# Low parts of four output-projection weight tiles made by DVE behind each feature tile's input parts, instead of by POOL

## Chip, cores and metric

One Trainium2 chip, one core. The metric is the device time of the kernel in microseconds (us), one launch.

## What is computed

One step of an encoder layer on 544 tokens (512 of new streams, 32 of running ones), D = 1024, all in float32: an input projection, sliding-window attention and gated linear attention, a merge, an output projection with a residual, then a SwiGLU feed-forward with a second residual. Cut to what matters here:

```python
def _merge(x, oa, ob, rb, ga, gb, g_ob, w_out):
    ob = _rmsnorm(ob, g_ob).reshape(B, T, D_MODEL) * jax.nn.silu(rb)
    m = jax.nn.sigmoid(ga) * oa + jax.nn.sigmoid(gb) * ob
    return x + m @ w_out                      # the output projection: the stage of the change

def _ffn(x, g, w_gate, w_up, w_down):
    h = _rmsnorm(x, g)
    return x + (jax.nn.silu(h @ w_gate) * (h @ w_up)) @ w_down
```

## The kernel before

Activations are kept transposed (features on the 128 partitions, 544 tokens along the free dimension). Every float32 product is made of three fast ones: each operand is split into a high part (fp32r) and a low part (what the rounding left), and TensorE adds high x high, high x low and low x high (function `chunk`, lines 654 to 656). A weight tile is 1024 x 128, stored as 128 x 1024. Tiles are numbered in the order of use: 0 to 52 are the input projection, 53 to 60 (`OUT0` = 53) the output projection, and from 61 (`GU0[0]`) come gate and up tiles in pairs for the feed-forward, whose products go by a scheme of sums of halves (`gate_up`, `first_gate_up`), and then down tiles.

A weight tile goes through a ring of 4 slots (`RING`): SyncE loads it into `wraw` (512 KB), ACT makes the high part `w_hi` (`high_part`, line 1066), and POOL or DVE makes the low part `w_lo` = `wraw` - `w_hi` (POOL in `lows`, line 594; DVE in `weight_low_part`, line 1786). Each low part adds 1 to the semaphore `w_split`. TensorE starts tile n when `w_split` is at least n + 1, and SyncE loads tile n only when the low part of tile n - 4 is counted (`raw_free`, line 445). So the load of tile 62, the first up tile, waits for the low part of tile 58. SyncE issues its loads in program order: 59, the residual rows of step 4, 60, residual 5, 61 (gate), residual 6, 62 (up), 63 (gate), residual 7, 64 (up).

DVE makes the low parts of tiles 4 to 33, POOL those of 1 to 3 and of 34 to 60 (and later of the down tiles).

The order of DVE's and ACT's work is written out by hand. In the output projection, step t (0 to 7) takes weight tile 53 + t and gives feature tile i = 0, 4, 1, 5, 2, 6, 3, 7 of the new residual x2T. On DVE a step is: add the residual to the PSUM result (line 1974), which also frees the PSUM bank; make the combinations for the feed-forward (`ffn_input`); and subtract ACT's high part (`f_low_part`, which waits for ACT twice in odd steps and once in even ones, and then counts `f_ok`). Even steps (i < 4) also add squares into `rv` (`add_squares`, line 1851). Step 4 begins, behind its residual add, with `first_sum(0)` (line 1892): it adds the two halves of up tile 62, so it waits for that load. From its result a chain runs over POOL's queue: an accumulating DMA (line 608), a second one (line 613), then ACT's high part of the sums (line 1097, in ACT's order behind step 5), then DVE's low part of them in step 6 (line 1903). Step 5 ends with a low part of tile 61, step 6 with `first_sum(1)`, step 7 holds the low part of tile 62.

TensorE goes through the eight tiles and then through `first_gate_up`: it starts when `f_ok` is 7, runs what needs the first seven feature tiles, and waits for `f_ok` = 8 before the rest.

Of the kernel before, what the change touches and what calls it, by code (L numbers as in the profile page):

```python
# [58 lines left out]
RING = 4  # L59
# [34 lines left out]
OUT0 = N_IN  # L94
OUT_ORDER = [0, 4, 1, 5, 2, 6, 3, 7]
FF_GROUPS = [8, 7, 7]
GU0, DN0 = [], []
# [30 lines left out]
def gemms(n):  # L128

    return sum(m not in PAIR_OF for m in range(n))  # L130


def uses_before(n):

    return sum(USES[m] for m in range(n % 2, n, 2))
# [12 lines left out]
HANDOVER = UNIT0 + 4  # L148
# [39 lines left out]
def mixer_program(nc, x_prompt, x_sample, cache_k, cache_v, state, w_in, w_a2, b_a, g_q, g_k, sinks,  # L188
                  g_ob, w_out, g_mix, g_ffn, w_gate, w_up, w_down,
                  y_prompt, y_sample, nk_p, nv_p, ns_p, nk_s, nv_s, ns_s):  # L190
    with ExitStack() as ctx:
        def sem(name):
            return ctx.enter_context(nc.semaphore(name))
# [141 lines left out]
        def halves(ps):  # L335

            return ps[:, :].rearrange("p (b n) -> p b n", b=2)[:, :, 0:TH]

        def h2(ap):

            return ap.rearrange("p (b n) -> p b n", b=2)
# [3 lines left out]
        w_split = sem("w_split")  # L345
# [228 lines left out]
        @block.gpsimd  # L574
        def _(pool):
            pool.memset(ident[:, :], 0.0).then_inc(pool_step, 1)
            pool.memset(cmask[:, :], 1.0).then_inc(pool_step, 1)
            pool.wait_ge(pool_step, 2)
            pool.affine_select(out=ident[:, :], in_=ident[:, :], compare_op=ALU.not_equal, fill=1.0,
                               base=0, pattern=[[-1, P]], channel_multiplier=1).then_inc(const_pool, 1)  # L580

            pool.iota(dist[:, :], pattern=[[-1, 2 * P]], base=P, channel_multiplier=1,
                      allow_small_or_imprecise_dtypes=True).then_inc(const_pool, 1)

            pool.affine_select(out=cmask[:, :], in_=cmask[:, :], compare_op=ALU.is_ge, fill=0.0,
                               base=0, pattern=[[1, P]], channel_multiplier=-1).then_inc(pool_step, 1)
            pool.wait_ge(pool_step, 3)
            cm = cmask[:, :].rearrange("p (b n) -> p b n", b=4)
            pool.affine_select(out=cm, in_=cm, compare_op=ALU.is_ge, fill=0.0, base=0,
                               pattern=[[-32, 4], [0, 32]], channel_multiplier=1).then_inc(const_pool, 1)  # L590

            def low_part(slot):

                pool.tensor_tensor(w_lo[:, slot, :, :], wraw[:, slot, :, :],  # L594
                                   w_hi[:, slot, :, :].bitcast(F32), ALU.subtract).then_inc(w_split, 1)

            def low_rank_low_part():

                pool.wait_ge(hi_done, 1)
                pool.tensor_tensor(w_hi[:, 0, :, RANK:2 * RANK], wraw[:, 0, :, 0:RANK],  # L600
                                   w_hi[:, 0, :, 0:RANK].bitcast(F32), ALU.subtract).then_inc(w_split, 1)

            def first_sums(q):

                r1 = (PAIRS[q][1] + 1) % RING
                pool.wait_ge(neg_ok, q + 1)
                pool.wait_ge(s1_ok, q + 1)
                pool.dma_start(wraw[:, r1, 0:HK, :], csum[q % 2][:, 1], accum_op=ALU.add).then_inc(s3_ok[q % 2], 16)  # L608

            def second_sum(q):  # L610

                pool.wait_ge(s3_ok[q % 2], 16 * (q // 2 + 1))
                pool.dma_start(csum[q % 2][:, 1], csum[q % 2][:, 0], accum_op=ALU.add).then_inc(s2_ok[q % 2], 16)

            def last_sum(q):

                pool.wait_ge(neg4_ok, q + 1)
                pool.wait_ge(s2_ok[q % 2], 16 * (q // 2 + 1))
                pool.dma_start(csum4[q % 2][:, :, :], csum[q % 2][:, 1], accum_op=ALU.add).then_inc(s4_ok, 16)

            def lows(ns):
                for n in ns:
                    pool.wait_ge(hi_done, gemms(n + 1))
                    low_part(n % RING)

            low_rank_low_part()
            lows(range(1, RING))
            pool.wait_ge(w_split, HANDOVER)
            lows(range(HANDOVER, GU0[0]))
            for g, m in enumerate(FF_GROUPS):  # L630
                q0 = FIRST[g]
                first_sums(q0)
                second_sum(q0)
                last_sum(q0)
                first_sums(q0 + 1)
                second_sum(q0 + 1)
                for q in range(q0, q0 + m):
                    if q + 2 < q0 + m:
                        first_sums(q + 2)
                    if q + 1 < q0 + m:  # L640
                        last_sum(q + 1)
                    if q + 2 < q0 + m:
                        second_sum(q + 2)
                lows(range(DN0[g], DN0[g] + KC))
# [824 lines left out]
        def _(dve):  # L1469
            steps = [0]  # L1470

            def link(ins):

                steps[0] += 1
                ins.then_inc(dve_step, 1)
                dve.wait_ge(dve_step, steps[0])
# [304 lines left out]
            def weight_low_part(m):  # L1781
                s = m % RING
                dve.wait_ge(hi_done, m + 1)
                if m == RING:
                    dve.wait_ge(w_split, RING)
                dve.tensor_tensor(w_lo[:, s, :, :], wraw[:, s, :, :], w_hi[:, s, :, :].bitcast(F32),  # L1786
                                  ALU.subtract).then_inc(w_split, 1)

# [8 lines left out]
            for n in range(N_IN):  # L1797
                if n == gate_tile(HEADS_B - 1) + 1:
                    empty_rows()
                if RING <= n + 2 < HANDOVER:  # L1800
                    weight_low_part(n + 2)
# [69 lines left out]
            def f_low_part(t, c):  # L1871
                dve.wait_ge(fin_ok, t + 1)
                if c < HK:
                    dve.wait_ge(f_hi_ok, t + 1)
                    dve.tensor_tensor(fa_lo[:, c], fin[:, 0:2], fa_hi[:, c].bitcast(F32), ALU.subtract)\
                        .then_inc(f_ok, 1)
                    return
                dve.wait_ge(f01_hi_ok, c - HK + 1)
                link(dve.tensor_tensor(fb_lo[:, c - HK, 0:2], fin[:, 0:2], fb_hi[:, c - HK, 0:2].bitcast(F32),
                                       ALU.subtract))  # L1880
                dve.wait_ge(f_hi_ok, t + 1)
                dve.tensor_tensor(fb_lo[:, c - HK, 2:5], fin[:, 2:5], fb_hi[:, c - HK, 2:5].bitcast(F32),
                                  ALU.subtract).then_inc(f_ok, 1)

            def first_sum(q):

                r1 = (PAIRS[q][1] + 1) % RING
                dve.wait_ge(wload[r1], 32 * ((PAIRS[q][1] + 1) // RING + 1))
                if q >= 2:
                    dve.wait_ge(pair_lo, 3 * (q - 1))  # L1890
                    dve.wait_ge(s2_ok[q % 2], 16 * (q // 2))
                dve.tensor_tensor(csum[q % 2][:, 0], wraw[:, r1, 0:HK, :], wraw[:, r1, HK:KC, :], ALU.add)                    .then_inc(s1_ok, 1)  # L1892

            def low_parts(q, k, at=None):

                _, n = PAIRS[q]
                dve.wait_ge(pair_hi, 3 * q + (k if at is None else at) + 1)
                if k < 2:
                    r = (n + k) % RING
                    lo, raw_w, hi = w_lo[:, r], wraw[:, r], w_hi[:, r]  # L1900
                else:
                    lo, raw_w, hi = c_lo[q % 2][:, :], csum[q % 2][:, :], c_hi[q % 2][:, :]
                dve.tensor_tensor(lo, raw_w, hi.bitcast(F32), ALU.subtract).then_inc(pair_lo, 1)  # L1903
# [66 lines left out]
            for t, i in enumerate(OUT_ORDER):  # L1970
                n = OUT0 + t
                dve.wait_ge(gemm_done, n + 1)
                dve.wait_ge(in_xres[t % XTS], 16 * (t // XTS + 1))
                dve.tensor_tensor(h2(x2T[:, i, :]), halves(G[n % 2]), h2(xTi[:, t % XTS, :]), ALU.add)\
                    .then_inc(set_free[n % 2], 1)
                dve.wait_ge(set_free[n % 2], uses_before(n) + 1)
                if t == HK:
                    first_sum(0)
                if t == 6:
                    low_parts(0, 2, 1)  # L1980
                if t == KC - 1:
                    low_parts(0, 1, 2)
                if i < HK and t:
                    add_squares(t - 1)
                ffn_input(i)
                f_low_part(t, i)
                if i < HK:
                    add_squares(t)
                if t == 5:
                    low_parts(0, 0)  # L1990
                if t == 6:
                    first_sum(1)
# [96 lines left out]
```

## Time and profile before

| | |
|---|---|
| median of 3 runs | 895.72 us (894.04 to 898.93) |
| the profiled execution, its own time | 896.06 us |
| span in the profile | 894.0 us |
| TensorE clock granted, mean | 0.998 |
| busy, share of span | PE 98%, weight load 95%, DVE 65%, ACT 46%, POOL 22% |

A timeline row has the start in us from the span's start, the duration, engine, line, operation, output and input, and in brackets how long the engine had been idle before and who released it. TensorE's matmuls are pipelined: one starts each 0.126 us though each is shown at 0.29 us. Two DVE instructions that don't depend on each other overlap by some 0.08 us, so the next one can start before the row's end. "busy (x)" in a table of windows is busy time and number of instructions.

### The profile page before, as it was taken

To read this page: it belongs to the slowest core of one execution; us is meant where nothing else is said; L and a number is where in the kernel's file an instruction comes from. 1 tells how busy PE (TensorE), PEld (TensorE's weight loads), DVE (VectorE), ACT (ScalarE), POOL (GpSimd) and SP (SyncE) were. 2 spreads that over 40 slices of the span, in tenths; PEclk is the share of its full clock that TensorE was granted. 3 is DMA by queue.
4 is the path that set the end of the run, shared out by engine and by line. 5 is a ranking of instruction groups with operands and counts; after the bars stand their busy time and mean duration, and the time that the engine had idled before them with its cause. 6 is when DMAs were issued, how large, how long until landed. Compare 5 with 4: busy or idle time off the path is not lost.

```text
span 894.0 us, 17248 instructions
## 1 busy us (share of the span) xinstructions
PE 875.1 (98%) x7061; PEld 848.2 (95%) x7061; DVE 579.7 (65%) x1156; ACT 414.0 (46%) x757; POOL 197.3 (22%) x131
## 2 busy tenths in 40 slices
PE   8989999999999999999999989999999999999998
PEld 7989999989998999999999989999999999999997
DVE  6773666676885436565556899973379853699722
ACT  6732443534554454545444575542155541366421
POOL 2200000000002323232324213235122153222350
PEclk9999999999999999999999999999999999999999
DMA  8531222121523121212107469853288723888322
GB/s 277 154 90 53 67 76 71 48 83 40 138 71 95 49 71 49 73 48 72 48 25 207 118 131 194 177 147 97 69 191 180 168 85 100 173 177 164 94 80 63
DMA packets 151028, 96.38 MB, mean 108 GB/s; under 512 B 5008, under 2 KB 140646, under 8 KB 150822
## 3 DMA queue, kind: packets, MB, share of 16 engines
q1 hardware_dynamic: 136326, 74.96, 29.3%
q0 software_dynamic: 9504, 17.31, 12.5%
q10 hardware_dynamic: 5120, 3.02, 1.2%
q8 instruction: 56, 0.92, 0.4%
q14 instruction: 22, 0.18, 0.1%
HBM read 71.45 MB, written 5.83 MB: 86 GB/s over the span
## 4 chain that ended last, share of the span: by engine, by line
PE 85%; DVE 9%; ACT 3%; issue 2%; DMA 2%; POOL 0%; DVEq 0%; SPq 0%; POOLq 0%
PE G L654 17%; PE G L656 16%; PE G L655 16%; PE X L933 4%; PE X L935 4%; PE X L936 4%; PE G L933 4%; PE G L935 4%; PE G L936 4%; PE X L864 2%; PE X L848 2%; PE X L833 2%; PE X L786 1%; PE X L774 1%; DVE w_lo L1786 1%
## 5 line engine op out<-in xcount | busy, mean ns | idle before, releaser
L654 PE MATMUL G<-h_hi,w_hi 128*128 128x272 f32 x1280 | 381.4, 298 | 3.4 <-DVE vB L1678 1.9
L656 PE MATMUL G<-h_hi,w_lo 128*128 128x272 f32 x1280 | 370.8, 290 | 0.0
L655 PE MATMUL G<-h_lo,w_hi 128*128 128x272 f32 x1280 | 369.2, 288 | 0.0
L654 PEld LDWEIGHTS G<-h_hi,w_hi 128*128 128x128 f32 x1280 | 241.6, 189 | 11.0 <-issue 7.0
L655 PEld LDWEIGHTS G<-h_lo,w_hi 128*128 128x128 f32 x1280 | 241.8, 189 | 0.8
L594 POOL TENSOR_TENSOR w_lo<-wraw,w_hi 128x1024 fp32r<-128x1024 f32 x54 | 138.4, 2570 | 470.7 <-DVE w_lo L1786 247.2
L656 PEld LDWEIGHTS G<-h_hi,w_lo 128*128 128x128 f32 x1280 | 241.3, 189 | 0.0
L1066 ACT ACTIVATE w_hi<-wraw 128x1024 fp32r<-128x1024 f32 (+1 forms) x129 | 134.5, 1045 | 60.6 <-PE G L656 35.2
L1266 ACT ACTIVATE prob<-prob,nm 128x256 f32<-128x256 f32 (+2 forms) x80 | 36.7, 460 | 64.4 <-DVE sd L1719 64.4
L2054 DVE TENSOR_TENSOR rs<-G,rv 128x544 f32<-128x544 f32 x23 | 16.7, 725 | 75.6 <-PE G L656 75.6
L1393 ACT ACTIVATE sq<-sq 128x544 f32<-128x544 f32 x22 | 14.5, 658 | 98.9 <-DVE sq L1941 98.9
L1903 DVE TENSOR_TENSOR w_lo<-wraw,w_hi 128x1024 fp32r<-128x1024 f32 x44 | 53.4, 1217 | 0.5 <-ACT w_hi L1066 0.5
L608 POOL DMA_DIRECT2D wraw<-csum x22 | 19.6, 889 | 111.5 <-DVE csum L1892 105.7
L933 PE MATMUL X<-fb,w_hi 128*128 128x272 f32 x144 | 41.5, 288 | 1.3 <-DVE up L1922 1.3
L935 PE MATMUL X<-fb,w_hi 128*128 128x272 f32 x144 | 41.5, 288 | 0.0
L936 PE MATMUL X<-fb,w_lo 128*128 128x272 f32 x144 | 41.5, 288 | 0.0
L1786 DVE TENSOR_TENSOR w_lo<-wraw,w_hi 128x1024 fp32r<-128x1024 f32 x30 | 36.3, 1216 | 2.7 <-ACT w_hi L1066 2.5
L933 PE MATMUL G<-fb,w_hi 128*128 128x272 f32 x120 | 34.8, 290 | 0.3 <-DVE up L1922 0.3
L935 PE MATMUL G<-fb,w_hi 128*128 128x272 f32 x120 | 34.7, 289 | 0.0
L936 PE MATMUL G<-fb,w_lo 128*128 128x272 f32 x120 | 34.6, 288 | 0.0
L1903 DVE TENSOR_TENSOR c_lo<-csum,c_hi 128x1024 fp32r<-128x1024 f32 x22 | 26.8, 1218 | 6.3 <-ACT c_hi L1097 6.2
L1726 DVE TENSOR_TENSOR den<-sm,es 128x4 f32<-128x4 f32 (+1 forms) x20 | 3.2, 160 | 41.8 <-ACT es L1268 41.8
(322 smaller groups left out, 1819.2 us busy)
## 6 DMA issues: line engine op xcount, KB each, us to landing
wraw<-in_w_in_dram SPq DMA_DIRECT2D x52, 512.0 KB
wraw<-in_w_gate_dram SPq DMA_DIRECT2D x22, 512.0 KB
wraw<-in_w_up_dram SPq DMA_DIRECT2D x22, 512.0 KB
csum<-csum POOLq DMA_DIRECT2D x44, 256.0 KB, 5.2
wraw<-in_w_down_dram SPq DMA_DIRECT2D x16, 448.0 KB
wraw<-csum POOLq DMA_DIRECT2D x22, 256.0 KB, 3.5
wraw<-in_w_out_dram SPq DMA_DIRECT2D x8, 512.0 KB
wraw<-in_w_down_dram SPq DMA_DIRECT2D x8, 512.0 KB
```

The costliest lines, as they stand in the source:

```text
L594: pool.tensor_tensor(w_lo[:, slot, :, :], wraw[:, slot, :, :], w_hi[:, slot, :, :].bitcast(F32), ALU.subtract).then_inc(w_split, 1)
L608: pool.dma_start(wraw[:, r1, 0:HK, :], csum[q % 2][:, 1], accum_op=ALU.add).then_inc(s3_ok[q % 2], 16)
L654: pe.matmul(o, w_hi[:, slot, kc, :], b_hi[:, kc, cols], start=(kc == 0), stop=False)
L655: pe.matmul(o, w_hi[:, slot, kc, :], b_lo[:, kc, cols], start=False, stop=False)
L656: mm = pe.matmul(o, w_lo[:, slot, kc, :], b_hi[:, kc, cols], start=False, stop=(kc == last))
L933: pe.matmul(bank, a_hi[:, kc, :], b_hi[:, kc, :], start=(kc == 0 and not adds), stop=False, skip_group_check=adds)
L935: pe.matmul(bank, a_hi[:, kc, :], b_lo[:, kc, :], start=False, stop=False, skip_group_check=adds)
L936: mm = pe.matmul(bank, a_lo[:, kc, :], b_hi[:, kc, :], start=False, stop=(kc == HK - 1), skip_group_check=adds)
L1066: act.activation(w_hi[:, n % RING, :, 0:m], wraw[:, n % RING, :, 0:m], ACT.Copy)\
L1266: act.activation(prob[0:nq, s, i, lo:hi], prob[0:nq, s, i, lo:hi], ACT.Exp, bias=nm[0:nq, s, i:i + 1], accum_out=sm[0:nq, s, i:i + 1])
L1786: dve.tensor_tensor(w_lo[:, s, :, :], wraw[:, s, :, :], w_hi[:, s, :, :].bitcast(F32), ALU.subtract).then_inc(w_split, 1)
L1903: dve.tensor_tensor(lo, raw_w, hi.bitcast(F32), ALU.subtract).then_inc(pair_lo, 1)
```

## The change

DVE makes the low parts of tiles 55 to 58 (steps 2 to 5), each two steps ahead of its use: behind `f_low_part` of step t it makes the one of tile 55 + t, for t = 0 to 3. POOL keeps 53 and 54, waits until `w_split` has counted 59, and then makes 59 and 60. DVE waits once, at tile 55, for POOL's count of 55, so that the counts keep their order.

```diff
@@ pool: order of the low parts
             pool.wait_ge(w_split, HANDOVER)
-            lows(range(HANDOVER, GU0[0]))
+            lows(range(HANDOVER, OUT0 + 2))
+            pool.wait_ge(w_split, OUT0 + 6)
+            lows(range(OUT0 + 6, GU0[0]))
@@ dve: weight_low_part
                 dve.wait_ge(hi_done, m + 1)
-                if m == RING:
-                    dve.wait_ge(w_split, RING)
+                if m in (RING, OUT0 + 2):
+                    dve.wait_ge(w_split, m)
@@ dve: for t, i in enumerate(OUT_ORDER)
                 ffn_input(i)
                 f_low_part(t, i)
+                if t < 4:
+                    weight_low_part(OUT0 + t + 2)
                 if i < HK:
                     add_squares(t)
```

## Rows read from the trace of the kernel before

**Rows 1.** The page: busy time of each engine
```profile
PE 875.1 (98%) x7061; PEld 848.2 (95%) x7061; DVE 579.7 (65%) x1156; ACT 414.0 (46%) x757; POOL 197.3 (22%) x131
```

**Rows 2.** Busy time by stretch (us; engine, busy, count; PEclk, DMA share, GB/s)
```profile
470.00:512.50 42.50, 42.50 (x340) 42.50 (x340) 30.92 (x45) 22.41 (x33) 14.03 (x8) 1.00 0.63 166
520.00:536.00 16.00, 14.00 (x103) 12.96 (x101) 15.29 (x25) 11.18 (x16) 2.58 (x3) 1.00 0.57 125
488.00:488.50 0.50, 0.50 (x6) 0.50 (x5) 0.00 (x0) 0.00 (x0) 0.50 (x1) 1.00 0.03 9
```

**Rows 3.** The chain that ended last, at the end of the first pair
```profile
520.86 0.71 DVE rv L1851
```

**Rows 4.** Timeline of TensorE: first matmul of steps 2, 3, first_gate_up, and the last part
```profile
476.37 0.29 PE L654 MATMUL G<-e_hi,w_hi 128*128 128x272 f32 x1
...
482.40 0.29 PE L654 MATMUL G<-e_hi,w_hi 128*128 128x272 f32 x1
...
512.57 0.29 PE L933 MATMUL G<-fa_hi,w_hi 128*128 128x272 f32 x1
...
518.98 0.28 PE L933 MATMUL G<-fb,c_hi 128*128 128x272 f32 x1
```

**Rows 5.** Timeline of POOL: low parts of tiles 56, 58, 59, 60, then a sum by DMA
```profile
468.98 2.44 POOL L594 TENSOR_TENSOR w_lo<-wraw,w_hi 128x1024 fp32r<-128x1024 f32 x1 [7.53 <-ACT w_hi L1066]
...
481.85 2.40 POOL L594 TENSOR_TENSOR w_lo<-wraw,w_hi 128x1024 fp32r<-128x1024 f32 x1 [3.67 <-ACT w_hi L1066]
487.44 2.70 POOL L594 TENSOR_TENSOR w_lo<-wraw,w_hi 128x1024 fp32r<-128x1024 f32 x1 [3.20 <-ACT w_hi L1066]
493.90 2.40 POOL L594 TENSOR_TENSOR w_lo<-wraw,w_hi 128x1024 fp32r<-128x1024 f32 x1 [3.76 <-ACT w_hi L1066]
497.46 1.00 POOL L608 DMA_DIRECT2D wraw<-csum  x1 [1.15 <-DVE csum L1892]
```

**Rows 6.** Instructions of line 1786, DVE's weight low parts: min/median/max ns
```profile
L1786 DVE TENSOR_TENSOR w_lo<-wraw,w_hi x30: 1197/1218/1226, 37.7 to 273.7; 128x1024 fp32r<-128x1024 f32 x30
```

**Rows 7.** Timeline of DVE in the output projection: ahead of step 0, and steps 0 to 7
```profile
469.08 2.36 DVE L1969 TENSOR_SCALAR param<-param 128x8 f32<-128x8 f32 x1
471.48 0.72 DVE L1974 TENSOR_TENSOR x2T<-G,xTi 128x544 f32<-128x544 f32 x1
...
476.57 0.72 DVE L1974 TENSOR_TENSOR x2T<-G,xTi 128x544 f32<-128x544 f32 x1 [1.48 <-PE G L656]
...
480.92 1.01 DVE L1882 TENSOR_TENSOR fb<-fin,fb 128x816 fp32r<-128x816 f32 x1 [0.26 <-ACT fb L1371]
482.61 0.72 DVE L1974 TENSOR_TENSOR x2T<-G,xTi 128x544 f32<-128x544 f32 x1 [0.68 <-PE G L656]
483.36 1.47 DVE L1851 TENSOR_TENSOR rv<-rv,sq 128x544 f32<-128x544 f32 x1
...
487.16 0.72 DVE L1851 TENSOR_TENSOR rv<-rv,sq 128x544 f32<-128x544 f32 x1
...
495.43 1.42 DVE L1892 TENSOR_TENSOR csum<-wraw 128x512 f32<-128x512 f32 x1
...
500.70 0.72 DVE L1974 TENSOR_TENSOR x2T<-G,xTi 128x544 f32<-128x544 f32 x1 [0.17 <-PE G L656]
...
507.11 0.72 DVE L1974 TENSOR_TENSOR x2T<-G,xTi 128x544 f32<-128x544 f32 x1
...
517.71 1.01 DVE L1882 TENSOR_TENSOR fb<-fin,fb 128x816 fp32r<-128x816 f32 x1 [0.26 <-ACT fb L1371]
```

**Rows 8.** Timeline of SyncE's queue: loads of tiles 57 and 58, and of 62
```profile
468.33 1.37 SPq L527 DMA_DIRECT2D wraw<-in_w_out_dram  x2
...
484.27 0.39 SPq L527 DMA_DIRECT2D wraw<-in_w_up_dram  x1
```

**Rows 9.** ACT in steps 0 and 5: a high part that waited for its load, and of the sums
```profile
474.62 1.06 ACT L1066 ACTIVATE w_hi<-wraw 128x1024 fp32r<-128x1024 f32 x1 [0.71 <-DMA wraw<-in_w_out_dram]
...
505.80 1.04 ACT L1097 ACTIVATE c_hi<-csum 128x1024 fp32r<-128x1024 f32 x1
```

## The prediction, made before the changed kernel had run

> **What bounds the kernel.** I read the page first, then busy time by stretch, the chain, and the timelines of the five queues in the 60 us in which the change works. TensorE is busy 98% of the span [rows 1], and in the output projection, from step 1 on, it is busy all of 42.50 us [rows 2]: no low part is late there, whoever makes it. After it the state changes: between 520 and 536 TensorE is busy 14.00 of 16 us and DVE 15.29 [rows 2], and from 520.86 the chain runs over DVE [rows 3]. So this stage has two clocks. TensorE takes a step in 482.40 - 476.37 = 6.03 us [rows 4]; DVE, with its waits for ACT, needs a little less in the first steps (idle 0.68 us before step 2) and hardly less later (0.17 before step 5, nothing before step 6) [rows 7]. DVE hands over to TensorE at `f_ok` = 8: its last instruction of step 7 ends at 517.71 + 1.01 = 518.72, TensorE reaches that point at 518.98 [rows 4, 7]. Only 0.26 us in hand; what makes DVE later than that moves the end, and as the chain stays with DVE behind it, nothing there takes it back.
>
> **What POOL loses.** Four low parts of 2.4 to 2.75 us. Nobody waits for them, so by itself this gives nothing. One effect on DVE is visible: a DVE instruction with its inputs in SBUF that meets a POOL low part lasts until that ends. The squares' sum at 483.36 took 1.47 us where 487.16 took 0.72, and POOL's ended at 484.25; the tiny one at 469.08 took 2.36 until POOL's end at 471.42; `first_sum(0)` took 1.42 until 496.85, POOL's ended at 496.30, so 0.55 after it [rows 5, 7]. The first two stretches vanish. They were in front of waits, so nothing is gained at the end (costed below).
>
> **What DVE gains: four low parts of 1.22 us [rows 6], effectively 1.14 in a row of instructions.**
> - Tile 55, behind step 0. Step 0 starts at 471.48 or earlier, its last input part ends by 474.7, so the low part ends by 475.9; step 2 needs it at 476.37 [rows 4, 7]. Cost 0. DVE was idle 1.48 us before step 1, which pays for it.
> - Tile 56, behind step 1. The input parts are through at 480.92 + 0.92 = 481.84, the low part ends at 483.05. TensorE's step 3 should begin at 482.40: it waits, with 0.1 for the start, **0.75 us**. DVE begins step 2 at 482.95 instead of 482.61.
> - Tile 57, behind step 2. An even step took 487.16 - 482.61 = 4.55, with the 0.75 that POOL held it; without, 3.8. So 482.95 + 3.8 + 1.2 = 487.95; TensorE needs it at 482.40 + 6.03 + 0.75 = 489.2. Cost 0.
> - Tile 58, behind step 3. An odd step takes 481.84 - 476.57 = 5.27. It starts when TensorE ends step 3, now 489.4; so 494.65 + 1.2 = 495.85 against a need at 495.2: again **0.75 us**. TensorE is now 1.5 behind.
>
> The waits at `hi_done` and at `w_split` = 55 are met long before, and POOL's 59 (from 495.9) and 60 (from 498.3), 2.4 each, are done at 498.3 and 500.7, ahead of steps 6 and 7 (502.0 and 508.0). Cost 0.
>
> **What the counts move on SyncE's queue.** The load of tile 62 waits for the low part of tile 58, today issued at 484.27, right when POOL ends (484.25) [rows 5, 8]. Now that low part ends at 495.85: the load goes out **11.6 us later**. Today's had its bytes moved by 488.0 with residual rows beside it, at most 3.7 us [rows 2, 8]; alone I take 3.3, so it lands at 499.2. Loads 59, 60, 61 are later too, but each lands before its high part; 63 and 64 go out at 498.4 and 500.8, needed at 511 and 517. The one who waits for tile 62 is DVE, at `first_sum(0)`, with all of steps 4 to 7 queued behind it.
>
> **Step 4.** DVE's residual add starts at 495.75 and needs no wait. Then it stands until 499.2, when POOL is in the middle of the low part of tile 60 and keeps the port until 500.7. `first_sum(0)` ends 0.55 later at 501.25 instead of 496.85: **4.4 us late**. The price of the landing lies between 3.0 us (then POOL's hold decides anyway) and the 6.2 that tile 57's load took from 468.33 to its high part at 474.6 behind four residual loads [rows 8, 9]; any landing between 498.7 and 500.7 gives the same time, and I take it for that reason.
>
> By the Trainium skill (SBUF — State Buffer, Who interferes with whom) whichever of DVE and GpSimd starts first holds the shared ports for its whole instruction and the other fully blocks. The rows agree; without the hold the sum would be 1.4 less, one of the rivals.
>
> **Steps 5 to 7.** Before step 5 DVE was idle 0.17 us and before 6 and 7 not at all, so the 4.4 shrinks by 0.17 and by a little where ACT had been the later one: step 5 starts at 504.85 (500.70), step 6 at 511.2 (507.11), the last input part ends at 522.8 (518.72), **+4.1**. The DMA chain on POOL's queue moves as one: line 608 from 497.46 to 501.9 (+4.4), so the high part of the sums in ACT's order from 505.80 to about 510, and step 6 needs its result at 512: 1 us to spare, which also covers ACT's queue behind that wait. TensorE ends step 7 1.5 late, stands some 2.3 us for `f_ok` = 7, works, and meets `f_ok` = 8 at 522.8 + 0.2 = 523.0 instead of 518.98: **+4.0 us**. The 1.5 lies inside this, not on top. `first_sum(1)` moves by 4.1 as well, so the next pair starts its sums no earlier relative to the rest.
>
> **Sum.** 0 (POOL) + 4.0 = 4.0 us. The profiled execution took 896.06 (span 894.0, 2.06 around it), so it would be 900.1; against the median of 895.72, which is 0.34 lower, 899.7: +0.45%. What a measurement here can tell from no change is about 0.5%, or 4.5 us, so this is **within it, on the slow side**.
>
> **Rivals.**
> 1. *Slower beyond 0.5%: the load of tile 62 lands after POOL's hold ends.* Place: `first_sum(0)`. Below 500.7 it costs nothing more; from there each us is one us at the end, and past +0.5 it leaves the band. With the 6.2 us of tile 57's load it lands at 502.05, the sum ends at 502.7, 5.9 late: +5.5 at the end, 901.2. For it: the load of 63 and residual rows follow it from 498.4. Against it: at its issue nothing is ahead of it in the queue, and today's took at most 3.7.
> 2. *Not held.* POOL and DVE slip past each other at 499.2, so `first_sum(0)` ends at 499.85: +2.6, 898.3. If the load were no wait at all, DVE would catch up with TensorE and only the two waits for tiles 56 and 58 stay: +1.5, 897.2. For it: small shifts decide who has the port. Against it: all three meetings in the rows were holds, and the load can't leave before 495.85.
> 3. *Faster, because the port is no longer shared.* DVE gets back 2.3 + 0.75 us, and a DVE instruction is half of POOL's. Were that on the path, it would give 895.72 - 3.0 = 892.7, and even this needs TensorE waiting for DVE before 512.5, where it had no idle at all. On the gains of this kind the Trainium skill (GPSIMD Engine Reference, Elementwise) has elementwise work with two inputs about twice as fast on VectorE. The trace agrees, 1.22 against 2.40, but at a place where nobody waits.
>
> **How the numbers follow.** The forecast 0.60, rival 1 0.17, rival 2 0.20, rival 3 0.03. The forecast's own spread, some 0.5 us of working and as much of measurement about +4.0, lies over 4.5 in 4 cases of 10: 0.24 to slower, 0.36 to within. So slower 0.17 + 0.24 = 0.41, rounded 0.40; faster 0.03; within 0.57. The range goes from the low end of rival 2, less 0.2 (897.0), to rival 1 with 1 us over it (902.2).
>
> **What would show it.** Right: four instructions of line 1786 between 474 and 496; TensorE idle some 0.75 us before steps 3 and 5, released by DVE's low part; the up load issued near 496; DVE idle about 3 us before `first_sum(0)`, and that instruction long, until POOL's end plus 0.55; TensorE idle about 2.3 us before `first_gate_up`; from there everything 4.0 later, with equal gaps. Wrong: no DVE idle at `first_sum(0)`; a load that lands after POOL; a gap behind 536 that closes or grows, which would say that the delay is taken back or paid again.

## The result, and the profile after the change

The changed kernel took a median of 902.08 us (898.94 to 903.63, 8 runs) against 896.52 (894.04 to 898.93, 8 runs) for the kernel before: the ratio is 1.0058, with a 95% interval of 1.0046 to 1.0070. By the ratio that is 5.2 us, 4.1 to 6.3. The forecast was +4.0 us, within 0.5% and "on the slow side", with 899.7 us and a range of 897.0 to 902.2. The time lies inside the range, near its end. But the ratio is above the half per cent, where the forecast had put 0.40; its likelier outcome, within the half per cent (0.57), did not come.

The profiled execution of the changed kernel took 901.81 us with a span of 899.7, 5.7 more than the span before. The page gives the busy time of each engine:

```profile
PE 877.7 (98%) x7061; PEld 850.0 (94%) x7061; DVE 578.5 (64%) x1160; ACT 414.1 (46%) x757; POOL 186.8 (21%) x127
```

DVE has four instructions more, and yet 1.2 us less of busy time than in [rows 1]. The added ones take 4.9 us; against them stand four instructions that POOL's low parts had stretched by 5.8 us in all. Three of them are in [rows 7] (2.19, 0.75 and 0.73 us too long). The fourth lies earlier, beside the low part of tile 55, in DVE's timeline before:

```profile
459.22 2.81 DVE L1772 TENSOR_TENSOR obT<-obT,gaT 128x544 f32<-128x544 f32 x1
```

The same instruction takes 0.72 us elsewhere. Busy time alone would have called the change a gain.

Busy time by stretch (the columns are those of [rows 2]), first the second stretch before, then both after:

```profile
512.50:520.00 7.50, 7.50 (x62) 7.50 (x61) 6.26 (x10) 5.99 (x11) 1.70 (x2) 1.00 0.60 125
```
```profile
470.00:512.50 42.50, 41.40 (x327) 40.96 (x327) 28.83 (x43) 20.41 (x30) 7.44 (x5) 1.00 0.54 149
512.50:520.00 7.50, 5.37 (x43) 5.18 (x42) 6.61 (x11) 4.08 (x8) 0.85 (x1) 1.00 0.58 111
```

TensorE was never idle in these stretches before; now it is, 1.1 us in the first and 2.1 in the second. The timeline of TensorE shows the three places, steps 3 and 5 of the output projection and the start of `first_gate_up`:

```profile
483.12 0.39 PE L656 MATMUL G<-e_hi,w_hi 128*128 128x272 f32 x1 [0.56 <-DVE w_lo L1788]
...
495.99 0.39 PE L656 MATMUL G<-e_hi,w_hi 128*128 128x272 f32 x1 [0.55 <-DVE w_lo L1788]
...
516.48 0.36 PE L935 MATMUL G<-fa_hi,w_hi 128*128 128x272 f32 x1 [2.13 <-issue]
```

(The row's idle time is a little under the loss, since the first matmul of a restart is longer (0.39 us against 0.29): from the last matmul at 482.27 to 483.12 it lost 0.72 us beyond its pace of 0.126. Waits of TensorE that are given in the text without a row include this, some 0.16 us. The third row names no releaser; the count it waits for, `f_ok` = 7, comes from DVE's input part of step 6, which ended at 516.37.)

The timeline of DVE in steps 3 to 5:

```profile
494.71 1.22 DVE L1788 TENSOR_TENSOR w_lo<-wraw,w_hi 128x1024 fp32r<-128x1024 f32 x1
495.85 0.72 DVE L1976 TENSOR_TENSOR x2T<-G,xTi 128x544 f32<-128x544 f32 x1
500.68 0.69 DVE L1894 TENSOR_TENSOR csum<-wraw 128x512 f32<-128x512 f32 x1 [4.12 <-DMA wraw<-in_w_up_dram]
...
504.97 0.72 DVE L1976 TENSOR_TENSOR x2T<-G,xTi 128x544 f32<-128x544 f32 x1
```

Here is the turn of the case: DVE stands for 4.12 us, and `first_sum(0)` ends at 501.37 instead of 496.85, 4.5 us late; step 5 starts at 504.97 instead of 500.70 [rows 7]. SyncE's queue says why the load was not there. It was issued at 495.96 instead of 484.27 [rows 8], when the low part of tile 58 was counted:

```profile
495.96 0.39 SPq L527 DMA_DIRECT2D wraw<-in_w_up_dram  x1
498.44 0.39 SPq L527 DMA_DIRECT2D wraw<-in_w_gate_dram  x1
```

and POOL's two low parts, which met DVE's wait:

```profile
496.01 4.75 POOL L594 TENSOR_TENSOR w_lo<-wraw,w_hi 128x1024 fp32r<-128x1024 f32 x2 [42.09 <-DVE w_lo L1788]
```

To follow the delay across kernels whose start differs by up to 2 us, I use one **measure** from here on: from TensorE's restart at the end of its wait near 468 to its restart behind the last wait of the second pair, near 537. These are the restarts before, and then after:

```profile
467.95 0.39 PE L654 MATMUL G<-h_hi,w_hi 128*128 128x272 f32 x1 [0.78 <-DVE h_lo L1777]
...
537.39 0.36 PE L933 MATMUL X<-fb,c_hi 128*128 128x272 f32 x1 [1.77 <-DVE c_lo L1907]
```
```profile
467.97 0.39 PE L656 MATMUL G<-h_hi,w_hi 128*128 128x272 f32 x1 [0.76 <-DVE h_lo L1779]
...
541.55 0.36 PE L935 MATMUL X<-fb,c_hi 128*128 128x272 f32 x1 [1.77 <-DVE c_lo L1909]
```

In the kernel before it is 537.39 - 467.95 = 69.44 us, in the changed one 541.55 - 467.97 = 73.58: **+4.14**. The stretch behind the measure holds the rest of the 5.7. Windows of the changed kernel (PEclk is the third column from the right):

```profile
540.00:542.00 2.00, 0.45 (x3) 0.48 (x4) 2.00 (x5) 1.11 (x2) 0.66 (x2) 1.00 0.56 155
542.00:544.00 2.00, 2.00 (x14) 2.00 (x13) 2.00 (x3) 0.00 (x0) 1.07 (x2) 0.69 1.05 218
544.00:546.00 2.00, 2.00 (x11) 2.00 (x10) 1.24 (x4) 0.66 (x1) 0.84 (x1) 0.50 1.04 143
546.00:548.00 2.00, 2.00 (x17) 2.00 (x17) 1.63 (x3) 1.64 (x3) 0.00 (x0) 0.96 1.08 269
```

TensorE was granted half its clock, 1.2 instead of 2.4 GHz, from about 542.8 to 546.2, behind a stretch in which it had waited 1.44 and 1.93 us. In the profile before, after waits of the same size, it kept 1.00 at this place:

```profile
540.00:542.00 2.00, 2.00 (x19) 2.00 (x18) 1.24 (x4) 0.92 (x3) 0.84 (x1) 1.00 1.06 141
542.00:544.00 2.00, 2.00 (x19) 2.00 (x18) 1.97 (x3) 2.00 (x5) 0.00 (x0) 1.00 1.09 280
```

A later matmul, one near 600, moved from 600.63 to 606.31, by 5.68, against 4.16 at the measure's end: the stretch at half clock cost 1.5 us.

### The profile page after: what moved, and what is told of

It is laid out like the page before. It is cut to its first block, busy times and chain, and to the rows that moved or that the text cites. A ratio compares the mean times of both kernels' runs of the same rounds, so it can differ in the third digit from the quotient of the medians.

```text
span 899.7 us, 17250 instructions
## 1 busy us (share of the span) xinstructions
PE 877.7 (98%) x7061; PEld 850.0 (94%) x7061; DVE 578.5 (64%) x1160; ACT 414.1 (46%) x757; POOL 186.8 (21%) x127
## 4 chain that ended last, share of the span: by engine, by line
PE 77%; DVE 11%; DMA 4%; issue 3%; ACT 3%; SPq 1%; POOL 0%; DVEq 0%; POOLq 0%
PE G L656 15%; PE G L658 14%; PE G L657 14%; PE G L935 4%; PE G L937 4%; PE G L938 4%; PE X L935 4%; PE X L937 4%; PE X L938 4%; PE X L866 2%; PE X L850 2%; PE X L835 2%; DMA csum<-csum 1%; DMA wraw<-in_w_in_dram 1%; DVE w_lo L1788 1%
## 5 line engine op out<-in xcount | busy, mean ns | idle before, releaser
L594 POOL TENSOR_TENSOR w_lo<-wraw,w_hi 128x1024 fp32r<-128x1024 f32 x50 | 128.0, 2568 | 486.3 <-DVE w_lo L1788 289.3
L1905 DVE TENSOR_TENSOR w_lo<-wraw,w_hi 128x1024 fp32r<-128x1024 f32 x44 | 53.4, 1217 | 0.8 <-ACT w_hi L1068 0.8
L1788 DVE TENSOR_TENSOR w_lo<-wraw,w_hi 128x1024 fp32r<-128x1024 f32 x34 | 41.2, 1217 | 2.7 <-ACT w_hi L1068 2.5
```

## The experiments

The theory, from the prediction: the delay comes over the **late load** of tile 62, for which DVE waits with four steps behind it. Rivals: DVE has too much work; TensorE's own waits for low parts; POOL's hold; and, new after the result, the granted clock.

### One low part alone

Only tile 58 goes to DVE, all others stay with POOL:

```diff
-            lows(range(HANDOVER, OUT0 + 2))
+            lows(range(HANDOVER, OUT0 + 5))
             pool.wait_ge(w_split, OUT0 + 6)
@@ dve: weight_low_part
-                if m in (RING, OUT0 + 2):
+                if m in (RING, OUT0 + 5):
                     dve.wait_ge(w_split, m)
@@ dve, behind f_low_part
-                if t < 4:
+                if t == 3:
                     weight_low_part(OUT0 + t + 2)
```

> DVE makes only the low part of tile 58 (behind step 3); POOL makes all others. The mark is the first matmul behind TensorE's last wait in the first pairs, 537.39 us in the kernel before and 541.55 after the change. Theory 'late load' (the load of tile 62 waits for the low part of 58, DVE waits for that load): one low part is enough for nearly all of the delay. Load issued near 495.1, first_sum(0) ends near 500.4, mark at 540.5 (+3.2). Rival 'DVE is overloaded' (four times 1.14 us of work): a quarter of the delay, mark near 538.4 (+1.0). Rival 'TensorE's waits for low parts': one wait of 0.75, mark at 538.1.

Measured: 901.11 us (4 runs), ratio 1.0048 (1.0034 to 1.0062). The measure is 541.02 - 467.60 = 73.42, +3.98. A quarter of the work makes nearly all of the delay, which leaves no room for a price by the amount of work, and TensorE has only one of its two waits. The size was higher than I expected (3.2), as SyncE's and DVE's timelines show:

```profile
494.78 0.39 SPq L527 DMA_DIRECT2D wraw<-in_w_up_dram  x1
```
```profile
500.14 0.69 DVE L1894 TENSOR_TENSOR csum<-wraw 128x512 f32<-128x512 f32 x1 [4.75 <-DMA wraw<-in_w_up_dram]
```

The load went out at 494.78 and DVE went on at 500.14, 5.4 us later, and half a microsecond after POOL's last low part had ended (494.83 + 4.76 = 499.59). So here the landing, not POOL, ended the wait.

### The other three

DVE makes 55, 56 and 57, POOL 58 as soon as 57 is counted:

```diff
-            pool.wait_ge(w_split, OUT0 + 6)
-            lows(range(OUT0 + 6, GU0[0]))
+            pool.wait_ge(w_split, OUT0 + 5)
+            lows(range(OUT0 + 5, GU0[0]))
@@ dve, behind f_low_part
-                if t < 4:
+                if t < 3:
                     weight_low_part(OUT0 + t + 2)
```

> DVE makes the low parts of 55, 56 and 57, POOL that of 58 at once when 57 is counted. Late load: the load of 62 goes out near 490.5 and is there before DVE wants it; only the wait for tile 56 (0.75 us) and POOL's hold for tile 60 are left, mark between +0.5 and +0.8. DVE overloaded: three quarters of the delay, +3.1.

Measured: 898.88 us (9 runs), ratio 1.0024 (1.0013 to 1.0036); the measure is 539.96 - 468.26 = 71.70, +2.26. Neither theory had the number. The load was no longer the cause (issued at 491.22, DVE's `first_sum(0)` at 497.55 did not wait for it). The timeline of DVE shows what took its place:

```profile
491.56 2.28 DVE L1867 SCALAR_TENSOR_TENSOR fin<-x2T,param,fin 128x272 f32<-128x272 f32 x1 [1.07 <-ACT fin L1362]
...
497.55 2.21 DVE L1894 TENSOR_TENSOR csum<-wraw 128x512 f32<-128x512 f32 x1
```

The first of them takes 0.50 us elsewhere, the second 0.69. POOL, let go once the low part of 57 was counted, ran two low parts in a row (488.38, 5.17 us for both) into the middle of step 3, and the third met `first_sum(0)`. The first hold is 1.8 us and new, the second 1.5 where it was 0.7 before [rows 7]. They are not the whole of it. Counted from each kernel's restart near 468 (468.26 here, 467.95 before), DVE was already 0.8 us late when it began step 3 (489.76 against 488.64), because TensorE had waited 0.7 us for tile 56, and `first_sum(0)` ended 2.6 us late. So the holds added 1.8 of the 2.6 there (the rest of what they took went into idle time), and 2.26 reached the measure's end. Where POOL's instruction falls matters as much as how long it is.

### The same four, one step earlier

```diff
-                if t < 4:
-                    weight_low_part(OUT0 + t + 2)
+                for m in ((2, 3), (4,), (5,))[t] if t < 3 else ():
+                    weight_low_part(OUT0 + m)
```

> The same four low parts on DVE, 55 and 56 behind step 0, 57 behind step 1, 58 behind step 2. Late load: the load of 62 goes out near 488, no low part is late for TensorE, mark at 537.4 (0.0, within 0.3). DVE overloaded: the work is the same, so the delay stays at 3 to 4 us. If the granted clock's drop comes with chance from one execution to the next, the time equals that of the kernel before within 1.5 us.

Measured: 896.44 us (12 runs), ratio 0.9995 (0.9984 to 1.0006). The measure is 535.62 - 466.17 = 69.45, +0.01. SyncE's and DVE's timelines:

```profile
486.27 0.39 SPq L527 DMA_DIRECT2D wraw<-in_w_up_dram  x1
```
```profile
493.65 1.70 DVE L1894 TENSOR_TENSOR csum<-wraw 128x512 f32<-128x512 f32 x1
```

DVE makes the same four low parts and nothing is lost: the load of 62 goes out at 486.27 (488 as expected, since this execution is 1.8 us ahead of the kernel before at its restart near 468), no low part is late for TensorE, and POOL's last one meets `first_sum(0)` as it did before (1.70 us for it). So neither DVE's 4.9 us of work nor the exchange of engines costs anything by itself; together with tile 58 alone, this puts the cost on the moment at which the low part of tile 58 ends. Nor does the change gain anything where it is well placed.

### DVE's wait without POOL

The change, with tiles 59 and 60 made by DVE too, inside its own wait:

```diff
             lows(range(HANDOVER, OUT0 + 2))
-            pool.wait_ge(w_split, OUT0 + 6)
-            lows(range(OUT0 + 6, GU0[0]))
@@ dve
                 if t == HK:
+                    weight_low_part(OUT0 + 6)
+                    weight_low_part(OUT0 + 7)
                     first_sum(0)
```

> The change, and tiles 59 and 60 also made by DVE, in the 4 us in which it stands before first_sum(0); POOL makes none of 55 to 60, so it holds no port there. If POOL's hold set the end of the wait: first_sum(0) starts where the load lands, 499.4 to 499.6, mark 1.2 earlier than after the change, 540.3. If the load's landing set it (it lands at 500.6, 4.7 us after its issue): first_sum(0) starts at 500.6 as before, mark at 541.5.

Measured: 901.25 us (6 runs), ratio 1.0046 (1.0030 to 1.0063); measure 541.33 - 467.88 = 73.45, +4.01. DVE's timeline:

```profile
495.78 0.72 DVE L1974 TENSOR_TENSOR x2T<-G,xTi 128x544 f32<-128x544 f32 x1
496.53 2.36 DVE L1786 TENSOR_TENSOR w_lo<-wraw,w_hi 128x1024 fp32r<-128x1024 f32 x2
500.40 0.69 DVE L1892 TENSOR_TENSOR csum<-wraw 128x512 f32<-128x512 f32 x1 [1.51 <-DMA wraw<-in_w_up_dram]
```

With no POOL instruction anywhere near, `first_sum(0)` still starts at 500.40, 4.5 us after the issue at 495.89. The landing ends the wait. In the changed kernel POOL's last low part ended at 500.76 and `first_sum(0)`, started at 500.68, took its plain 0.69 us: it was not held, and POOL's end only happened to fall on the same moment. Two instructions of 1.2 us in that wait cost nothing, a second sign that DVE has time there.

### Four idle subtractions on top of the kernel before

```diff
                 f_low_part(t, i)
+                if t < 4:
+                    dve.tensor_tensor(csum[1][:, :].rearrange("p a k n -> p (a k n)"),
+                        e_hi[:, :, :].rearrange("p a n -> p (a n)")[:, 0:2 * TH + 480].bitcast(F32),
+                        e_lo[:, :, :].rearrange("p a n -> p (a n)")[:, 0:2 * TH + 480].bitcast(F32),
+                        ALU.subtract)
```

> The kernel before, POOL making all its low parts, and four extra subtractions of 128x1024 on DVE behind the input parts of steps 0 to 3, of the size of a low part, whose results nobody reads. Measure: from TensorE's restart at the end of its one wait near 468 to its restart behind the last wait near 537 (before 69.44 us; after the change 73.58). Late load: nothing waits for these four, the load of 62 goes out by 485.5; POOL's holds meet DVE more often, so +0.5 to +2.0. DVE overloaded: the same work as in the change, so +4.

The four results are read by nobody. Measured: 902.75 us (4 runs), ratio 1.0077 (1.0057 to 1.0097); the measure is 544.06 - 467.97 = 76.09, +6.65. I expected 0.5 to 2. DVE's timeline:

```profile
483.74 2.18 DVE L1851 TENSOR_TENSOR rv<-rv,sq 128x544 f32<-128x544 f32 x1
...
489.39 2.92 DVE L1851 TENSOR_TENSOR rv<-rv,sq 128x544 f32<-128x544 f32 x1
...
499.36 2.15 DVE L1892 TENSOR_TENSOR csum<-wraw 128x512 f32<-128x512 f32 x1
```

The extra work itself is small, but it makes DVE and POOL meet in every step: three instructions of about 0.7 us took 2.2, 2.9 and 2.15, together 5.1 us too long (two of them were held before, for 0.75 and 0.73, so 3.6 is new). The holding went both ways: POOL's low parts of tiles 58, 59 and 60 took 3.49, 3.19 and 3.48 us, where they took 2.40, 2.70 and 2.40 before [rows 5]. Step 5 began at 505.10, as late as in the changed kernel, though load 62 had gone out at 485.37. The granted clock was at half from about 515.4 to 522.2, in and behind a wait of TensorE of 4.0 us, and that is in the measure too. So this run doesn't show that DVE's work is harmless; it shows that extra work beside POOL's low parts costs as much as the late load. That four instructions of this size are harmless where they replace POOL's is what the earlier placement shows.

### The late load alone

The kernel before, one wait added on SyncE's queue:

```diff
                 gate_weights(0, i)
                 residual(XTS + 2 + i)
+                if i == 0:
+                    sp.wait_ge(f_ok, 4)
                 up_weights(0, i)
```

> The kernel before, POOL making all its low parts, with one wait more: SyncE issues the load of tile 62 only behind the input parts of step 3 (near 494). No work is added to DVE, no low part is late. Late load: this alone makes most of the delay; the load lands 4.4 to 5.8 us after its issue as in the changed kernels, first_sum(0) ends near 499.5 instead of 496.85, and TensorE's restart behind the last wait near 537 moves by 2.3 to 3.8 us against its restart near 468 (69.44 before, so 71.7 to 73.2). Rival (DVE's four instructions and TensorE's two waits are needed for it): no move beyond 0.5.

The wait holds back what SyncE issues behind it too: the load of 63 went out at 494.60 (490.17 before), followed by residual rows. Measured: 899.46 us (7 runs), ratio 1.0039 (1.0023 to 1.0055). No instruction moved between engines, no low part was late, and DVE stands as in the changed kernel. SyncE's and DVE's timelines:

```profile
494.16 0.39 SPq L527 DMA_DIRECT2D wraw<-in_w_up_dram  x1
```
```profile
499.81 0.69 DVE L1894 TENSOR_TENSOR csum<-wraw 128x512 f32<-128x512 f32 x1 [4.27 <-DMA wraw<-in_w_up_dram]
```

`first_sum(0)` ends at 500.50 instead of 496.85, 3.65 later. The measure is 542.01 - 468.10 = 73.91, +4.47, more than that, as the clock was at half behind the 2.9 us wait before `first_gate_up`:

```profile
514.00:516.00 2.00, 0.39 (x2) 0.42 (x3) 1.21 (x2) 1.97 (x3) 0.00 (x0) 0.92 0.00 0
516.00:518.00 2.00, 2.00 (x11) 2.00 (x11) 1.97 (x4) 0.73 (x3) 0.71 (x1) 0.50 0.03 8
518.00:520.00 2.00, 2.00 (x14) 2.00 (x14) 1.93 (x4) 1.84 (x4) 0.15 (x1) 0.73 0.75 112
```

What this costs can be read off. From the restart before `first_gate_up` to the measure's end, the changed kernel, the runs with tile 58 alone, with the other three and without POOL take 25.07 to 25.10 us; this run takes 542.01 - 515.61 = 26.40. So 1.3 us of the +4.47 are the clock and 3.2 the late load. That is 1.0 less than the +4.14 of the changed kernel, because the load went out 1.8 us earlier and took 0.9 longer. (With the idle subtractions the same stretch took 27.45: 2.4 of its +6.65 are the clock.) The late load is enough for the delay; the wait it makes is then a candidate for a slow clock.

### The clock: waits filled with idle matmuls

Each execution comes with its mean granted clock, and the times lie in steps with it. Of the kernel before, the comparisons with the experiments hold 61 executions: nine at 1.000 (median 894.67 us), 38 at 0.998 (896.52), ten at 0.996 (898.09), four others. The step from 1.000 to 0.998 is a stretch at half clock behind a 2 us wait near 55, which the profiles of both kernels have. These are the windows before:

```profile
58.00:60.00 2.00, 2.00 (x11) 2.00 (x11) 1.85 (x3) 1.99 (x4) 0.00 (x0) 0.54 0.44 134
60.00:62.00 2.00, 2.00 (x13) 1.99 (x12) 0.73 (x1) 0.22 (x1) 0.00 (x0) 0.61 0.04 10
```

The profiled execution of the earlier low parts, at a mean of 1.000, had the same wait and kept its clock:

```profile
58.00:60.00 2.00, 2.00 (x19) 1.99 (x18) 1.97 (x3) 1.93 (x3) 0.00 (x0) 1.00 0.26 78
```

The pair of waits at the end of the measure, 1.3 and 1.8 us in the rows, is the same in eight profiles in which nothing fills it. Behind it the clock fell in three (the changed kernel, tile 58 alone, the late load) and stayed up in five.

In 13 of 61 the clock of the kernel before was 0.996 or 0.995; in the changed one in six of eight. First the two waits of the second pair were filled in the changed kernel (`keep_busy` runs products of ones into columns that nobody reads):

```diff
+                if q == 1:
+                    keep_busy(G[0][:, 288:288 + P], 4)
                 pe.wait_ge(evicted, 6 * q + 2)
                 product(b7, w_hi[:, r1, k2], w_lo[:, r1, k2], fb_hi[:, :, 4], fb_lo[:, :, 4], adds=True)
+                if q == 1:
+                    keep_busy(G[0][:, 288:288 + P], 6)
                 pe.wait_ge(evicted, 6 * q + 3)
```

> The change, and 4 and 6 idle matmuls on TensorE into an unused part of a PSUM bank in its two waits of the second pair (near 536 and 540), shorter than the waits. Clock theory: part of the 5.2 us is no wait but the granted clock at half behind these waits, in most executions of the change and in a quarter of those of before; with the waits filled it does not fall there, the measure stays at +4.1, the mean granted clock rises from 0.996 to 0.998 or more, and the time falls by 1 to 1.6 us. Rival (the clock has nothing to do with it): time as after the change, 902.

Measured: 901.35 us (6 runs), ratio 1.0054 (1.0038 to 1.0070): inconclusive on the time. The measure was 544.27 - 468.23 = 76.04, +6.60 and not +4.1 as expected. The clock stayed at 1.00 from 536 to 548, but in this profile it was at half from about 519.2 to 522.7, behind the wait before `first_gate_up`, which was 3.4 us long here, since `first_sum(0)` started only at 502.04, 5.8 us after the load's issue. (The stretch from the restart at 517.84 to the measure's end took 26.43, so 1.3 us of it are the clock; the rest of what it has over the changed kernel is the longer landing.) Two executions at 0.999 took 899.31 (median), three at 0.997 901.76. So one stretch was avoided and another came in its place.

Then all waits filled, in three kernels. The fills of the second pair, and

```diff
+                if n == 5:
+                    pe.wait_ge(z_free, HEADS_B)
+                    keep_busy(X[1][:, 832:832 + P], 6)
                 if n >= 2:
                     pe.wait_ge(set_free[n % 2], uses_before(n))
```

on top of the early low parts and on top of the kernel before; and in the changed kernel also, ahead of `first_gate_up`,

```diff
+                keep_busy(X[0][:, 288:288 + P], 8)
                 pe.wait_ge(set_free[1], uses_before(n))
                 pe.wait_ge(f_ok, KC - 1)
```

> Low parts one step earlier (as in e3), the two waits of the second pair filled as in e7, and 6 idle matmuls in TensorE's 2 us wait near 55, behind which the granted clock is at half at 58 to 62 in most executions. Clock theory: mean granted clock 1.000, 894.4, which is what the undisturbed executions of e3 took; 2.4 less than the kernel before. Rival: the idle matmuls change nothing or delay what waits behind them, 896.4 or more.

> The kernel before with the same three fills. Clock theory: 894.4, as the executions of before at a mean clock of 1.000 (894.2). If the early low parts are worth nothing, e8 and e9 are equal within 0.3 us.

> The change with the fills of e8 and 8 idle matmuls more in the wait before first_gate_up (2.3 us). Clock theory: mean granted clock 0.999 or more, and against the filled kernel before (894.4) only the waits are left, 4.2 to 5: 898.5 to 899.4; so the clock had 2.5 to 3.5 us of the 902.1. Rival (no part of the clock): 900 to 901.5.

| kernel | median us (runs) | ratio to before, 95% | measure |
|---|---|---|---|
| early low parts, filled | 894.65 (11) | 0.9980 (0.9970 to 0.9989) | 69.44 |
| before, filled | 894.36 (11) | 0.9977 (0.9969 to 0.9986) | 69.45 |
| changed, filled | 898.96 (9) | 1.0031 (1.0019 to 1.0043) | 73.58 |

All executions of the three had a mean clock of 0.999 or 1.000. One execution of the first took 4823.73 us at a mean clock of 1.000, and nothing on record explains it; its ten others lie between 893.42 and 895.78, and the ratio is theirs. The wait near 55, filled in the kernel before:

```profile
54.68 1.50 PE L673 MATMUL X<-ones 128*128 128x128 f32 x12
56.61 0.40 PE L654 MATMUL G<-h_hi,w_hi 128*128 128x272 f32 x1 [0.43 <-DVE vB L1685]
```

(the row counts each of the six idle products twice), and its windows:

```profile
56.00:60.00 4.00, 3.57 (x29) 3.39 (x28) 3.81 (x8) 2.67 (x4) 0.00 (x0) 1.00 0.48 131
60.00:64.00 4.00, 4.00 (x35) 3.99 (x33) 2.71 (x4) 0.68 (x2) 0.00 (x0) 1.00 0.47 135
```

Against the kernel before, the filled kernels gain 0.23% and 0.20%, 2.1 and 1.8 us, and are the fastest here; the low parts' place makes no difference between them. The filled changed kernel still has its waits, 1.0031 / 0.9977 = 1.0054 against the filled kernel before, about 4.8 us by the ratios and 4.6 by the medians, and +4.13 in the profiled measure. Its expectation (898.5 to 899.4) held, as did the 894.4 for the other two within 0.3; the fills took 2.4 us from the changed kernel and 2.1 from the one before. So of the 5.2 us the waits hold 4.1 to 4.8, and the change's own part of the clock is the difference of these gains, some tenths of a microsecond in the median, which these intervals can't tell from nothing. In the one profiled execution of the result it was 1.5.

## Why the prediction was right, and where it was not

- *No low part was late before, and TensorE has no slack to give.* Right [rows 2]. The changed kernel's TensorE idles at the two steps named, 3 and 5, by 0.72 and 0.71 us where 0.75 was forecast; tiles 55 and 57 were in time.
- *The 1.5 us lie inside the delay, not on top.* Right: with one such wait instead of two (tile 58 alone) the measure was +3.98 against +4.14, and in both `first_sum(0)` ended late by nearly the same, counted from the start of the measure.
- *The load of 62 goes out 11.6 us later and DVE stands at `first_sum(0)`.* Right, and the cause: issued at 495.96 (forecast 495.85), and the late load alone makes `first_sum(0)` end 3.65 us late, where the change makes 4.5.
- *POOL's hold decides when `first_sum(0)` runs.* **This step failed**, though its number came out, 501.37 for the end against 501.25. That is luck: a landing 1.4 us later than the one taken, and no hold. The prediction had named the row that would show it, a long `first_sum(0)` behind an idle of about 3 us; the row has 0.69 us behind 4.12. I took 3.3 us from issue to landing, from a window by whose start the bytes of the load before had moved [rows 2, 8], and so believed that POOL's low part of tile 60 set the time. Without POOL it began at the same moment, 4.5 us after the issue. The windows of the changed kernel show why:

```profile
498.00:499.00 1.00, 1.00 (x11) 1.00 (x10) 0.00 (x0) 0.00 (x0) 1.00 (x2) 1.00 1.06 315
499.00:499.50 0.50, 0.50 (x7) 0.50 (x6) 0.00 (x0) 0.00 (x0) 0.50 (x1) 1.00 0.23 66
```

  As much as the load's 512 KB (524 thousand bytes) had moved by about 499.3, where the last column falls to 66 GB/s, and still DVE went on only at 500.68: the end of the bytes is not the landing. The profiled landings were 4.5 to 5.8 us (495.89 to 500.40, 495.96 to 500.68, 494.78 to 500.14, 494.16 to 499.81, 496.22 to 502.04, and 4.6 in the changed, filled kernel). The bytes don't make this spread. These are the 3.4 us behind the issue in the changed kernel (landing 4.7 us) and in the one with the second pair filled (5.8):

```profile
495.96:499.36 3.40, 3.37 (x27) 3.38 (x28) 0.60 (x1) 0.66 (x1) 3.35 (x2) 1.00 0.54 155
```
```profile
496.22:499.62 3.40, 3.37 (x27) 3.37 (x28) 0.61 (x1) 0.66 (x1) 3.34 (x2) 1.00 0.52 153
```

  That is 527 and 520 thousand bytes, one load's worth in both. (A window counts the bytes of all loads together, so that the last of this load's are among them is not shown.) As each microsecond of it beyond POOL's end is one at the end, this spread belongs to the time; it was in the text as rival 1, with 6.2 us as its end, and the forecast's own landing band (498.7 to 500.7) just held the 500.68.
- *Everything after moves as one by 4.0.* Right up to the end of the second pair: step 5 starts at 504.97 (forecast 504.85), step 6 at 511.36 (511.2), the wait before `first_gate_up` was 2.29 (2.3), and the measure +4.14. The sums had their 1 us to spare: ACT's high part ran at 510.19 and step 6 did not wait.
- *Faster, since the port is free.* The held stretches went as forecast (the instruction at 469.1 fell from 2.36 to 0.17 us; so did the fourth, at 459.22, which the prediction had not seen), and the earlier placement shows what it is worth at the end: +0.01 in the measure, ratio 0.9995.
- *What the sum lacked.* The clock. The prediction has no term for it; the rows before showed a granted value of 1.00 in this part. By their mean clock, 13 of 61 executions of the same kernel have a second stretch at half clock. In the profile this is the gap that grows behind 536, from 4.16 to 5.68, one of the signs of being wrong that the prediction had named.
- *From 899.7 to 902.08.* 0.8 of these 2.4 us lie in the kernel before: the forecast stood on a median of 895.72 from three executions, and over eight it is 896.52. The rest is the +4.0 against 5.6 by the medians (5.2 by the ratio).

The two rivals in steady supply, an overloaded DVE and POOL's hold, are each real, but elsewhere: DVE's work costs when POOL's runs beside it (+6.65 with the idle subtractions, clock included), and the holds are some 1.8 of the 2.6 us by which `first_sum(0)` ended late in the kernel with three low parts moved.

What stays open: how the spread of 4.7 us between the changed kernel's executions divides between landing and clock, as only profiled executions show the landing; and why the landing takes 4.7 us in one execution and 5.8 in another, when as many bytes have moved 3.4 us after the issue in both. The shortest (4.5) is that of the kernel in which POOL does nothing then; a single execution doesn't show that this is why. POOL may not be needed for the long ones: with the late load alone it was idle from 496.5 on, and the landing took 5.65. But there the load of 63 followed 0.4 us behind instead of 1.9 to 2.5, so that run has another reason of its own.

## What to carry to other kernels

Before moving an operation to another engine or later, look up which counts it feeds: a ring of buffers turns "two steps ahead of its use" into "the moment at which the slot's next load may start", and that load has its own reader. Here the reader wanted it at 495.43 [rows 7], so that with a landing of 4.5 to 5.8 us the low part of tile 58 was due between 489.6 and 490.9, some 4 to 5 us before TensorE wanted it (482.40 + 2 x 6.03 = 494.46 [rows 4]). Give the operation its place by the earlier of the two due times; one step earlier, the same change cost nothing. And price a load by rows in which someone waited for it, not by when its bytes stopped moving.

## What I had not expected of the hardware

- A load of 512 KB released its reader 4.5 to 5.8 us after its issue, though as many bytes had moved after 3.3 to 3.5 us: 1.4 us before the release in the changed kernel, 2.3 in the one with the second pair filled.
- The granted clock of TensorE fell to half for about 3.4 us behind some waits of 2 to 3.4 us, and behind two of 1.4 and 1.9 us close together, and for 6.8 us in and behind one of 4.0; it did not fall behind others of the same size. A stretch of 3.4 us cost 1.3 us (26.40 against 25.1 between two fixed restarts) to 1.9 (the step between the medians at 1.000 and 0.998). The Trainium skill (TensorE: Matmul & The Clock Gate, The HAM clock gate) says that the window over which activity is watched is free-running and that the same kernel therefore shows a different number of slow matmuls from run to run. The 61 executions of the kernel before agree: by their mean clock the same program has one such stretch mostly, none in nine and two in 13.
- Idle matmuls in waits of 1.3 to 2.3 us, shorter than the waits, kept the clock up: 0.999 or more in 31 of 31 executions, and 2 us less for a kernel in which nothing else had changed.
